# Two chained blocks on one Trainium2 core: the 64x64 inversions on four quadrants instead of two, with the identity kept in the running inverse

## The reference

```python
a_mat = jnp.where(tri_strict, jnp.einsum('nbhid,nbhjd->nbhij', kb, kc) * decay, 0.0)
eye = jnp.eye(cs, dtype=jnp.float32)
t_mat = lax.linalg.triangular_solve(eye + a_mat, jnp.broadcast_to(eye, a_mat.shape),
                                    left_side=True, lower=True, unit_diagonal=True)
u = jnp.einsum('nbhij,nbhjd->nbhid', t_mat, vb)
w = jnp.einsum('nbhij,nbhjd->nbhid', t_mat, kb * jnp.exp(gcum)[..., None])
```

```python
sa = jnp.einsum('bhvk,bhk->bhv', S, kk_t)
S = (S * w_t[:, :, None, :] - sa[..., None] * (kk_t * a_t)[:, :, None, :]
     + v_t[..., None] * k_t[:, :, None, :])
```

## Time and profile before

| what | value |
|---|---|
| median of 3 runs (lowest, highest) | 2830.95 us (2829.75, 2832.68) |
| span of the profiled execution | 2824.7 us |
| median less span | 6.25 us |
| busy share: PE, DVE, ACT, POOL | 89%, 52%, 32%, 21% |
| the four inversion stages together | 259.43 us |

### The profile page before, as it was taken

One profiled execution on the slowest core, in us unless ns is written; L12 is line 12 of the kernel. 1 busy time (PEld: TensorE's weight loads), 2 busy tenths in 40 slices (PEclk: granted clock), 3 DMA queues, 4 the chain that ended last, 5 costly groups with the idle time before them and its releaser, 6 DMA issues. The chain is left out here.

```text
span 2824.7 us, 59589 instructions
## 1 busy us (share of the span) xinstructions
PE 2503.6 (89%) x25174; PEld 2090.7 (74%) x25174; DVE 1460.0 (52%) x2544; ACT 904.8 (32%) x1456; POOL 598.1 (21%) x311
## 2 busy tenths in 40 slices
PE   7967697796968899888978999999988998999998
PEld 3856585684955788677867888888876775688886
DVE  6787686546457855355552443034215464742341
ACT  3243224214043433512233322122224443332232
POOL 0000000110112222010004223222331200644444
PEclk9987697897989999999989999999998999999999
DMA  7521151000033733000031112112214202422232
GB/s 276 180 88 46 37 191 42 3 4 2 4 121 105 246 101 119 33 3 2 4 120 60 52 67 67 60 59 66 70 63 162 76 1 72 172 96 99 89 105 81
DMA packets 63137, 229.29 MB, mean 81 GB/s; under 512 B 6352, under 2 KB 12880, under 8 KB 60880
## 3 DMA queue, kind: packets, MB, share of 16 engines
q1 hardware_dynamic: 62928, 226.22, 23.2%
HBM read 211.52 MB, written 13.63 MB: 80 GB/s over the span
## 5 line engine op out<-in xcount | busy, mean ns | idle before, releaser
L2347 POOL TENSOR_TENSOR b_wl<-b_stage,b_wh 128x1024 fp32r<-128x1024 f32 (+1 forms) x72 | 186.6, 2591 | 475.8 <-ACT b_wh L2343 475.8
L2646 DVE SCALAR_TENSOR_TENSOR f_xr<-f_ps,cols,f_xr 128x511 f32<-128x511 f32 (+1 forms) x132 | 83.2, 658 | 327.5 <-ACT f_xr L2639 327.5
L2343 ACT ACTIVATE b_wh<-b_stage 128x1024 fp32r<-128x1024 f32 (+1 forms) x72 | 81.5, 1132 | 459.5 <-PE f_ps L2478 404.9
L2347 POOL TENSOR_TENSOR c_wl<-c_stage,c_wh 128x1024 fp32r<-128x1024 f32 (+1 forms) x68 | 182.4, 2683 | 213.0 <-ACT c_wh L2343 213.0
L2478 PE MATMUL f_ps<-h_h,b_wl 128*128 128x256 f32 (+1 forms) x672 | 226.3, 337 | 0.0
L2478 PE MATMUL f_ps<-h_h,b_wh 128*128 128x256 f32 (+1 forms) x672 | 226.1, 336 | 0.0
L2478 PE MATMUL f_ps<-h_l,b_wh 128*128 128x256 f32 (+1 forms) x672 | 225.8, 336 | 0.0
L2343 ACT ACTIVATE c_wh<-c_stage 128x1024 fp32r<-128x1024 f32 (+1 forms) x68 | 77.3, 1137 | 256.1 <-PE f_ps L2478 232.5
L2478 PEld LDWEIGHTS f_ps<-h_h,b_wh 128*128 128x128 f32 x672 | 127.5, 190 | 13.7
L2347 POOL TENSOR_TENSOR a_wl<-a_stage,a_wh 128x1024 fp32r<-128x1024 f32 x33 | 84.9, 2572 | 248.1 <-ACT a_wh L2343 248.1
L2478 PEld LDWEIGHTS f_ps<-h_h,b_wl 128*128 128x128 f32 x672 | 127.6, 190 | 13.2
(11 more groups left out here) (721 smaller groups left out, 6626.2 us busy)
## 6 DMA issues: line engine op xcount, KB each, us to landing
b_stage<-in_ffn_up SPq DMA_DIRECT2D x44, 512.0 KB, 3.3
c_stage<-in_ffn_up SPq DMA_DIRECT2D x44, 512.0 KB, 3.3
first_stage<-in_w_in SPq DMA_DIRECT2D x33, 512.0 KB, 3.6
a_stage<-in_ab_w SPq DMA_DIRECT2D x25, 512.0 KB, 3.6
p_hgrn_side_w<-in_ada_w SPq DMA_DIRECT2D x12, 1024.0 KB, 5.0
b_stage<-in_ffn_down SPq DMA_DIRECT2D x16, 704.0 KB, 4.0
c_stage<-in_ffn_down SPq DMA_DIRECT2D x16, 704.0 KB, 4.0
a_in_side_w<-in_ada_w SPq DMA_DIRECT2D x8, 1024.0 KB, 7.1
```

Source lines behind the costliest of these rows:

```text
L2343: self.nc.scalar.activation(self.wh[:, slot, :w], self.stage[:, slot, :w], ACT.Copy).then_inc(self.w_high, 1)
L2347: self.nc.gpsimd.tensor_tensor(self.wl[:, slot, :w], self.stage[:, slot, :w], self.wh[:, slot, :w].bitcast(F32), ALU.subtract).then_inc(se ...
L2646: nc.vector.scalar_tensor_tensor(out, b[:, :n - 1], self.tap(part, 0, i), out, ALU.mult, ALU.add).then_inc(self.before_ok[part], 1)
```

## The change

The tiles of a stage come in units now: 12, 8, 8 and 8 tiles in an rwkv stage, three times 8 in a gdn stage. Half of each unit's tiles stay on the straight pieces, with bank `x` of the unit; the other half multiply on the crossed pieces, with bank `y`. The crossed tiles keep `lower` and `part` (the given matrix) on their own partitions and `cx` and `upper` on the far ones: the first product crosses over, and the second crosses back. PE's stream takes a straight and a crossed tile in turn. The transposes of the setup all stay straight.

The identity is kept in `cx`: POOL copies it in at the start, and after the second products of levels 1 to 3 copies it back into the columns that the level overwrote. With it the second products give the whole new columns of `lower` and `upper`, and what were additions become copies: DVE copies those of the straight bank, ACT those of the crossed bank, in three instructions a unit, since `upper` needs one for each half of the partitions. DVE's picks are predicated copies instead of multiplications by the mask. In the setup ACT fills `upper` and `lower` with the identity, DVE puts the level-0 blocks in by predicated copies, and ACT copies the crossed tiles' `upper` over to the far partitions. In the gdn stages `on_act` is called behind each step instead of in a loop ahead of level 5. The number of matmuls and their sizes stay.

The diff, cut: removed lines stand only where a call or a signature changes (the others are in the listing above).

```diff
-def inverses64(nc, t, name, lt, xt, n_groups, d, beside=None):
...
+def inverses64(nc, t, name, parts, d, beside=None):
+    ends = list(np.cumsum([part.shape[1] for part in parts]))
+    n_parts, n_tiles = len(parts), int(ends[-1])
+    n_of = [part.shape[1] // 2 for part in parts]
+    at_step = {(u, lv): n for n, (lv, u) in enumerate((lv, u) for lv in range(1, 6) for u in range(n_parts))}
...
+        def first_half(u):
+            return slice(int(ends[u]) - 2 * n_of[u], int(ends[u]) - n_of[u])
+        def second_half(u):
+            return slice(int(ends[u]) - n_of[u], int(ends[u]))
+        def both(u):
+            return slice(int(ends[u]) - 2 * n_of[u], int(ends[u]))
...
+        def out_of(bank, u, part, lv):
+            n = n_of[u]
+            return bank[:, 32 * n * part:32 * n * part + 32 * n].rearrange("p (a m s) -> p a m s", a=n, s=1 << lv)
         @block.gpsimd
         def _(pool):
...
+            for lv in (1, 0):
+                for u in range(n_parts):
+                    nc.gpsimd.tensor_copy(cx[:, lv, both(u)], spread(ident, 1, 2 * n_of[u])).then_inc(unit, 1)
             for lv in range(1, 4):
...
+                for u in range(n_parts):
+                    pool.wait_ge(product2, at_step[u, lv] + 1)
+                    old = columns_of(cx[:, lv % 2, both(u)], lv, d)
+                    new = one(ident, lv, d)
+                    nc.gpsimd.tensor_copy(old, spread(new, 1, 2 * n_of[u])).then_inc(unit, 1)
         @block.vector
         def _(dve):
...
+            for u, part in enumerate(parts):
+                n = n_of[u]
+                dve.wait_ge(filled, 2 * u + 2)
+                first = spread(m64[:, M64[f"level0_{d}"], :], 1, n).bitcast(int32)
+                nc.vector.copy_predicated(upper[:, first_half(u)], first, part[:, :n, :]).then_inc(placed, 1)
+                nc.vector.copy_predicated(lower[:, second_half(u)], first, part[:, n:, :]).then_inc(placed, 1)
             for lv in range(1, 6):
...
+                rows = t["maskrow"][:, M32[f"row{lv}_{d}"], :].rearrange("p (m s) -> p m s", s=1 << lv)
+                for u in range(n_parts):
+                    step = at_step[u, lv]
+                    dve.wait_ge(product1, step + 1)
+                    dve.wait_ge(unit, step + 1)
+                    where = spread(rows, 1, n_of[u]).bitcast(int32)
+                    for half, bank in ((first_half(u), straight[u]), (second_half(u), across[u])):
+                        nc.vector.copy_predicated(columns_of(cx[:, lv % 2, half], lv, d), where, out_of(bank, u, 0, lv)
+                                                  ).then_inc(picked, 1)
+                for u, part in enumerate(parts):
+                    step = at_step[u, lv]
+                    dve.wait_ge(product2, step + 1)
                     if lv < 5:
...
+                        nc.vector.tensor_copy(columns_of(lower[:, first_half(u)], lv, d), out_of(straight[u], u, 1, lv))
+                        nc.vector.tensor_copy(columns_of(upper[:, first_half(u)], lv, 1 - d), out_of(straight[u], u, 0, lv)
+                                              ).then_inc(straight_ok, 1)
                     else:
...
+                        nc.vector.tensor_copy(columns_of(part[:, :n_of[u], :], lv, 1 - d), out_of(straight[u], u, 0, lv))
                     if beside is not None:
...
+                        beside.on_dve(dve, step)
         @block.scalar
         def _(act):
...
+            for u in range(n_parts):
+                for half, to in ((first_half(u), upper), (second_half(u), lower)):
+                    nc.scalar.activation(to[:, half], spread(ident, 1, n_of[u]), ACT.Copy).then_inc(filled, 1)
+            for u in range(n_parts):
+                act.wait_ge(placed, 2 * u + 2)
+                for c in range(2):
+                    nc.scalar.activation(upper[rows64(c), second_half(u)], lower[rows64(1 - c), second_half(u)], ACT.Copy
+                                         ).then_inc(crossed, 1)
+                act.wait_ge(turned, u + 1)
+                act.wait_ge(crossed, 2 * u + 2)
+                for half, bank in ((first_half(u), straight[u]), (second_half(u), across[u])):
+                    ins = nc.scalar.activation(lower[:, half], bank[:, :C * n_of[u]].rearrange("p (a t) -> p a t", t=C), ACT.Copy)
+                ins.then_inc(crossed_ok, 1)
+            for lv in range(1, 6):
+                for u, part in enumerate(parts):
+                    step = at_step[u, lv]
+                    if lv == 5:
+                        n = n_of[u]
+                        act.wait_ge(product1, step + 1)
+                        act.wait_ge(straight_ok, at_step[u, 4] + 1)
+                        act.wait_ge(crossed_ok, n_parts + at_step[u, 4] + 1)
+                        nc.scalar.activation(columns_of(part[:, :n, :], lv, d), columns_of(upper[:, first_half(u)], lv, d), ACT.Copy)
+                        for c in range(2):
+                            nc.scalar.activation(columns_of(part[rows64(1 - c), n:, :], lv, d),
+                                                 columns_of(upper[rows64(c), second_half(u)], lv, d), ACT.Copy)
+                    act.wait_ge(product2, step + 1)
+                    if lv < 5:
+                        nc.scalar.activation(columns_of(lower[:, second_half(u)], lv, d), out_of(across[u], u, 1, lv), ACT.Copy)
+                        got = out_of(across[u], u, 0, lv)
+                        for c in range(2):
+                            ins = nc.scalar.activation(columns_of(upper[rows64(c), second_half(u)], lv, 1 - d), got[rows64(1 - c)],
+                                                       ACT.Copy)
+                        ins.then_inc(crossed_ok, 1)
+                    else:
+                        nc.scalar.activation(columns_of(part[:, n_of[u]:, :], lv, 1 - d), out_of(across[u], u, 0, lv), ACT.Copy)
+                    if beside is not None:
+                        beside.on_act(act, step)
         @block.tensor
         def _(pe):
...
+            def each(u):
+                for a in range(n_of[u]):
+                    for crossing in range(2):
                         for c in range(2):
...
+                            tile = a + n_of[u] * crossing
+                            yield a, tile, int(ends[u]) - 2 * n_of[u] + tile, (across if crossing else straight)[u], \
+                                rows64(c), rows64(c ^ crossing)
+            open_clock_with(nc, t, across[-1], 2)
+            for u in range(n_parts):
+                pe.wait_ge(placed, 2 * u + 2)
+                for a, _, tile, bank, own, _ in each(u):
+                    src = upper if bank is straight[u] else lower
+                    done = nc.tensor.matmul(bank[own, a * C:(a + 1) * C], src[own, tile, :], ident[own, :], start=True, stop=True)
                 done.then_inc(turned, 1)
             for lv in range(1, 6):
...
+                for u, part in enumerate(parts):
+                    n = n_of[u]
+                    pe.wait_ge(crossed_ok, at_step[u, lv] + 1)
+                    if lv > 1:
+                        pe.wait_ge(straight_ok, at_step[u, lv - 1] + 1)
+                    for a, i, tile, bank, own, far in each(u):
+                        done = nc.tensor.matmul(bank[far, a * 32:a * 32 + 32], part[own, i, :], one(lower[own, tile, :], lv, d),
                                                 start=True, stop=True)
                     done.then_inc(product1, 1)
...
+                for u in range(n_parts):
+                    n = n_of[u]
+                    pe.wait_ge(picked, 2 * at_step[u, lv] + 2)
                     if lv < 5:
...
+                        for a, _, tile, bank, own, far in each(u):
+                            nc.tensor.matmul(bank[own, (n + a) * 32:(n + a) * 32 + 32], upper[far, tile, :],
+                                             one(cx[far, lv % 2, tile, :], lv, d), start=True, stop=True)
+                    for a, _, tile, bank, own, far in each(u):
+                        done = nc.tensor.matmul(bank[own, a * 32:a * 32 + 32], cx[far, lv % 2, tile, :],
+                                                one(upper[far, tile, :], lv, 1 - d), start=True, stop=True)
                     done.then_inc(product2, 1)
                     if beside is not None:
...
+                        beside.on_pe(pe, at_step[u, lv])
...
-            inverses64(nc, t, f"rwkv{d}_inv", four, four, 9, d)
+            inverses64(nc, t, f"rwkv{d}_inv", [w["early"][:, :, 0, :], *(w["late"][:, 8 * u:8 * u + 8, 0, :] for u in range(3))], d)
...
-            inverses64(nc, t, f"gdn{d}_inv", four, four, TT, d, GdnRest(nc, t, d, rows, qkv[:, 0:GW, :], w, dec))
+            inverses64(nc, t, f"gdn{d}_inv", [w["lt"][:, 8 * u:8 * u + 8, :] for u in range(3)], d,
+                       GdnRest(nc, t, d, rows, qkv[:, 0:GW, :], w, dec))
```

More of the change, by code:

```diff
@@ L1297, in _ @@
+            for lv in range(1, 4):
+                for u in range(n_parts):
[3 more added lines that the diff above has]
```

(9 more changed lines are left out.)

99 lines of the change are left out of this document (10 added, 89 removed).

## The result

The changed kernel takes 2810.4 us in the median of 4 runs (2800.86 to 2813.06), the kernel before 2830.35 in 4 runs: a ratio of 0.993, with an interval of 0.991 to 0.995. It is faster by 0.7%, 20 us where 95.8 were forecast, and outside the range. The time is near that of the rivals in which passes stay at 29 ns (2817) or the clock stays low (2805). The first does not have the cause; the low clock is a part of it, in the rwkv stages. The profiled run took 2800.86 us, the fastest of the four, for a span of 2799.0, so 1.9 us lie around a span. The 6.25 us counted for that before were mostly a difference between runs, which the forecast, a difference of spans, did not use.

The account below looks back on a forecast made before the run. PE, busy 89% of the span, was taken to bound the kernel. Inversion stages: 2 x 39.7 + 2 x 36.6 = 152.6 us against 259.4, so 106.8 less, minus 8 (clock) and 3 (contention): 2830.95 - 95.8 = 2735 us, range 2708 to 2785.

Parts of the forecast that it names:

- the low clock: Rival for the inversion stages: clock stays at the lower level throughout, 26.8 ns a pass, 2805 us in all; chance 0.04.
- The 6.25 us: Whole kernel: difference between the profiled execution's span and the median of the runs, taken to stay.
- What bounds the kernel: Whole kernel: PE, busy 89% of the span, is what the inversions wait for; those four stages take 259.43 us.
- Four pieces: Matmuls of the inversion stages: all four pieces work at once, 14.6 ns a pass in place of 29.1.
- 27.3 + 2.4: rwkv levels: 1872 passes at 14.6 ns are 27.3 us, then 2.4 us of ACT's copies at the end.
- Setups: Start of the stages: ACT's copies and evictions bound it, 10.0 us in rwkv and 7.2 in gdn.
- Tail: End of a stage: ACT's last copies and evictions show, 2.4 us in rwkv and 1.6 in gdn.
- gaps: gdn levels: PE waits behind DVE's operations of 1.75 us, 2.9 us a stage, between 0 and 10.
- The slower rival: Inversion stages: POOL's short-run copies bound them, slower than before from 8.8 ns a column; chance 0.06, 0.035 of it beyond break-even.
- Clock: Inversion stages: thin PE work in the setup lowers the clock in the first level, 2 us a stage, 8 in all.
- A floor under the distance of any two starts: Rival: 32-column passes can't start as close as 15.8 ns; at 22.5 ns the run takes 2778 us; chance 0.02.
- pieces take turns: Rival: PE runs crossed and straight pairs alternately, passes stay at 29.1 ns, only setup gains, 2817 us; chance 0.06.

Follow-up runs that it names:

- e4: The changed kernel run again as it was, on another chip: 2810.2 us, ratio 0.9928 to the kernel before.
- e1: Kernel before plus a stage in which only PE works, in series of 640 passes: 32 columns took 16.60 us on four pieces, 18.80 on two.
- e7: The changed kernel with seven full 256-column matmuls added in each gdn stage, rwkv still on four pieces: 2791.7 us, ratio 0.9887 to the kernel before.
- e2: The changed kernel with the crossed tiles put back on the straight pieces: 2810.1 us, ratio 0.9944 to the kernel before.
- e8: Kernel before plus a second set of PE-alone series (nops, two pauses, full weights, 64 columns): 32 columns on four pieces took 16.7 us, 64 columns 16.2.
- e9: Kernel before plus PE-alone series with semaphore increments behind matmuls: 49 us on four and on two pieces; four pieces without increments 17.00 us.

## Why the prediction was wrong

**What bounds the kernel.** Right, as far as it went: PE was dense and nobody held it up. That a straight piece's 58 ns set the rate was right too, but the next limit lay close behind it. No row was asked for that, though the trace of before has it, in the scan behind the first inversion stage (windows, with columns as above):

```profile
617.71:621.36 3.65, 2.37 (x127) 2.24 (x128) 1.24 (x4) 1.15 (x4) 0.00 (x0) 1.00 0.02 4
...
625.27:629.19 3.92, 2.37 (x128) 2.29 (x128) 2.03 (x7) 0.60 (x2) 0.00 (x0) 1.00 0.03 6
```

These are 127 and 128 passes at full clock in 3.65 and 3.92 us, some 30 ns each, with 1.4 and 1.6 us of waiting on "issue" behind them. It is the rate that the changed stages then had.

**Four pieces: the step that failed.** "I take 14.6 ns a pass" was right as a distance (14.4 to 14.6 in the bursts) and wrong as a rate. The row it came from, 96 passes of the scores, is shorter than the stock of 158 to 230 passes with which PE's series began. Beyond it 128 passes came each 3.5 to 4.0 us, 27 to 31 ns a pass. In the first rwkv stage the levels took 60.71 us for 2026 passes, 30.0 ns each, where the sum had 27.3 + 2.4 behind the first products. A second term was too small beside it: the clock, priced at 2 us a stage, was at its lower level for some 56 of these 60.71 us, with passes 26.7 ns apart while they ran.

**Where the 76 us that are missing lie.** The stages were to be 152.6 and are 229.0, or 232.4 in e4. rwkv has 56 of it (135.5 for 79.4): nothing in it lasts long for few instructions. There the two limits lie upon each other: PE's own distance at the low clock, 26.7 ns, is nearly all of the 30, and the waits on "issue" are the rest. That supply would have held it near this rate at the full clock is read from e1 and from e7's group of 128 passes in 3.45 us; no run had an rwkv stage on four pieces at full clock throughout. gdn has 20 (93.5 for 73.2): there eight long matmuls, 6.7 us by the sum, give the supply time, and the four pieces use it up after. I take that to be the 5 to 8 us between e2's gdn stages and the change's.

**Setups.** Near: the first second product began 10.5 us into the rwkv stage and 8.1 into the gdn stage, where 10.0 and 7.2 were counted to that point. DVE's predicated copies beside POOL took 0.84 to 1.06 us for 256 columns, not the 0.44 of the earlier trace rows, and the setups still came out within 1 us.

**Tail, gaps, POOL.** ACT's tail is about 1.3 us and not 2.4, as a slower PE would leave it; PE's weight loads waited for DVE's picks 1.2 us in the first gdn stage where 2.9 were counted; POOL at 1.6 ns a column never held a pick up. The slower rival needed 8.8.

**Clock.** Its fall was foreseen, its length not: the rwkv levels ran at 0.54 on average and not only in level 1. But three equal series, at 1.00, 0.72 and 0.76, took 16.6, 16.7 and 17.0 us (e1, e8, e9), which speaks for a small cost within the stages. Behind them the stretches to the next inversion are longer than before, 2.2 us behind the first rwkv stage and 3.7 behind the first gdn stage in the first profile. These two and 2.4 behind the second gdn stage are over a quarter of the 29.4 that the stages gave. In e4, whose time is that of the median, all that lies between and behind the four stages is 14.7 us longer than in the profile of before, over half of the 26.0 that its stages gave. The low clock at their starts (0.50 and 0.67 over the first 6 us in the first profile) has a part in this: behind the first rwkv stage 42 passes stand where 132 stood. How large a part wasn't measured. The first inversion also began 3.7 us earlier in this profile; that start lies between 527 and 532 in all runs so that no effect of the change can be read from it.

**Rivals.** "A floor under the distance of any two starts" is refuted at 14.6 ns; "pieces take turns" had the time and not the mechanism. The low clock had its sign, 27 ns at 0.5, in both rwkv stages, though these took 66.7 and 68.8 us and not its 61; in the gdn stages groups of 128 passes stalled at the full clock. (The 2805 for it is not quite what its stages of 61 and 52 add up to: 2801 less only the contention, 2809 with both terms.) The instructions were on no list, though the page before showed a queue for them in its third part.

Open: why the clock fell for nearly all of the rwkv stages and in two of three equal series of PE alone; what an rwkv stage on four pieces takes at full clock; and how much the transfers' own wait could be shortened. None of these was tried. That instructions are what each group of 128 passes waits for rests on their number and on the transfers between the groups; no run changed the number of instructions alone.

## What to carry to other kernels

Count instructions as well as passes: many small matmuls in a row didn't run faster than their instructions arrived, here 256 each 3.5 to 4.0 us, some 29 ns for a weight load and a matmul. A short burst in a trace shows the distance of passes, not a rate that lasts; look for a series longer than the stock, and for waits on "issue" at equal counts. Where such a stretch waits for instructions at the full clock, long matmuls can lie in its waits: seven in a gdn stage cost nothing and kept the clock up. Where the clock had already fallen, in rwkv, fifteen of them cost 12 us a stage. Four pieces paid only where long matmuls already stood between.

## What the runs showed of the hardware that was not expected

- PE alone on four pieces stalled every 128 passes, with one 16 KB transfer on the instruction queue for each group and 0.9 to 1.9 us of waiting on "issue" before it at the full clock; 158 to 230 passes of 32 columns and 206 of 64 ran before the first stall.
- A fall to the lower clock halfway cost a series on four pieces next to nothing: 16.7 us at 0.72 and 17.0 at 0.76, 16.6 at 1.00.
- A semaphore increment behind each matmul raised a pass from 14.6 ns (four pieces) and 29.2 (two) to 56 to 60 alike at the full clock, and to 77 over the series (0.54 and 0.53), while 80 of them among 20 matmuls of 512 columns left these as long as they were (17.4 us for 40 passes).
